# The doubling inverse of a chunked recurrence changes partition halves at some levels, and its turned update is issued between state and output products

## What is computed

```python
def rwkv7_scan(S0, r, decay, k, v, a_vec, b_vec):
    def step(S, inp):
        r_t, w_t, k_t, v_t, a_t, b_t = inp
        sa = jnp.einsum('bhvk,bhk->bhv', S, a_t)
        S = S * w_t[:, :, None, :] + sa[..., None] * b_t[:, :, None, :] + v_t[..., None] * k_t[:, :, None, :]
        return S, jnp.einsum('bhvk,bhk->bhv', S, r_t)
    xs = tuple(jnp.swapaxes(t, 0, 1) for t in (r, decay, k, v, a_vec, b_vec))
    S, ys = lax.scan(step, S0, xs)
    return jnp.swapaxes(ys, 0, 1), S
```

## Time and profile before

| what | us |
| --- | --- |
| median of 3 runs | 4411.86 |
| lowest, highest | 4408.74, 4422.03 |
| span of the profiled execution | 4419.8 |
| PE busy in it | 3990.1 (90%) |
| DVE busy in it | 2070.8 (47%) |
| ACT busy in it | 1727.3 (39%) |

### The profile page before, as it was taken

The page is one execution under the profiler, slowest core; times in us unless marked ns, Lnnn a source line. Parts: engine busy times, 40 slices in busy tenths (PEclk is TensorE's granted clock), DMA queues, the critical chain, the costliest instruction groups (busy, mean ns, idle before and its releaser), DMA issues.

```text
span 4419.8 us, 113544 instructions
## 1 busy us (share of the span) xinstructions
PE 3990.1 (90%) x49138; PEld 3475.0 (79%) x49138; DVE 2070.8 (47%) x4539; ACT 1727.3 (39%) x3547; POOL 519.2 (12%) x273
## 2 busy tenths in 40 slices
PE   7999999899968888879989999998999688888798
PEld 7999999788865565558989999997888565655587
DVE  6111112688845555555231111136787455565465
ACT  3000001577756665552110000026777465665421
POOL 5222221000000000002032222210000000000111
PEclk9999999999989999999999999999999899999899
DMA  3111112111124354344321111121111243543532
GB/s 141 73 63 73 73 73 79 46 52 52 37 59 148 112 177 135 91 145 153 112 72 73 73 73 73 69 81 40 51 48 37 81 158 90 176 139 108 175 128 79
DMA packets 227845, 410.47 MB, mean 93 GB/s; under 512 B 32786, under 2 KB 136980, under 8 KB 214292
## 3 DMA queue, kind: packets, MB, share of 16 engines
q1 hardware_dynamic: 213236, 320.15, 23.0%
q10 hardware_dynamic: 14112, 83.07, 4.7%
HBM read 296.39 MB, written 106.76 MB: 91 GB/s over the span
## 4 chain that ended last, share of the span: by engine, by line
PE 69%; DVE 10%; ACT 9%; issue 5%; PEld 3%; SPq 2%; DMA 2%; POOL 0%; ACTq 0%; DVEq 0%; PEldq 0%
PE psum L2251 11%; PE psum L2254 11%; PE psum L2253 11%; PE psum L1419 5%; PE psum L1447 4%; PE psum L762 3%; PE psum L1435 2%; PE psum L1183 2%; ACT arena L1223 2%; PE psum L1753 2%; PE psum L1754 2%; PE psum L1755 2%; PE psum L833 1%; PE psum L1175 1%; PE psum L759 1%
## 5 line engine op out<-in xcount | busy, mean ns | idle before, releaser
L2251 PE MATMUL psum<-x_hi,w_parts 128*128 128x416 f32 x2640 | 933.0, 353 | 42.8 <-POOL w_parts L2134 18.6
L2254 PE MATMUL psum<-x_hi,w_parts 128*128 128x416 f32 x2640 | 934.6, 354 | 0.0
L2253 PE MATMUL psum<-x_lo,w_parts 128*128 128x416 f32 x2624 | 918.5, 350 | 0.0
L2150 DVE TENSOR_TENSOR arena<-psum,arena 128x416 f32<-128x416 f32 x330 | 195.0, 592 | 1196.1 <-PE psum L2254 1192.3
L2251 PEld LDWEIGHTS psum<-x_hi,w_parts 128*128 128x128 f32 x2640 | 498.0, 189 | 52.6 <-POOL w_parts L2134 20.3
L375 ACT ACTIVATE arena<-arena 128x256 f32<-128x256 f32 x16 | 8.0, 501 | 1329.4 <-POOL arena L2138 1329.4
L2253 PEld LDWEIGHTS psum<-x_lo,w_parts 128*128 128x128 f32 x2624 | 494.9, 189 | 8.9 <-issue 0.6
L2254 PEld LDWEIGHTS psum<-x_hi,w_parts 128*128 128x128 f32 x2640 | 497.3, 188 | 3.4
L1326 DVE TENSOR_SCALAR_CACHE_REDUCE arena<-psum 128x512 f32<-128x512 f32 (+3 forms) x640 | 357.5, 607 | 287.7 <-PE psum L1419 155.3
L1419 PE MATMUL psum<-arena 64*128 64x512 f32 (+3 forms) x1280 | 329.4, 619 | 41.1 <-DVE arena L1326 22.4
L1447 PE MATMUL psum<-arena 128*128 128x128 f32 x2176 | 307.1, 282 | 64.0 <-ACT arena L1232 46.8
(11 more groups left out here) (348 smaller groups left out, 6754.8 us busy)
## 6 DMA issues: line engine op xcount, KB each, us to landing
arena<-in_cache_k SPq DMA_DIRECT2D x256, 256.0 KB, 2.9
arena<-in_cache_v SPq DMA_DIRECT2D x256, 256.0 KB, 3.0
out_proj_t<-arena ACTq DMA_DIRECT2D x60, 1040.5 KB, 4.1
arena<-in_w_in SPq DMA_DIRECT2D x66, 512.0 KB, 3.5
arena<-out_proj_t SPq DMA_DIRECT2D x96, 257.0 KB, 3.5
arena<-out_proj_t SPq DMA_DIRECT2D x24, 1024.0 KB, 6.2
x_res<-in_x SPq DMA_DIRECT2D x10, 1664.0 KB, 12.4
m_raw<-mixed_t SPq DMA_DIRECT2D x8, 1664.0 KB, 10.8
```

Of the source, the lines that this page charges most:

```text
L2150: dve.tensor_tensor(ost[:, b % 2, 1 + g * TG:1 + (g + 1) * TG], bank[PB[q % 7]][:, 0:TG], RSTD[:, cols(g)], ALU.mult).then_inc(p_ev, 1)
L2251: pe.matmul(bank[PB[q % n]][:, 0:TG], w_hi[:, b % 3, k, :], x_hi[:, g, k, :], start=(k == 0), stop=False)
L2253: pe.matmul(bank[PB[q % n]][:, 0:TG], w_hi[:, b % 3, k, :], xl, start=False, stop=False)
L2254: mm = pe.matmul(bank[PB[q % n]][:, 0:TG], w_lo[:, b % 3, k, :], x_hi[:, g, k, :], start=False, stop=(k == KT - 1))
```

## The change

It does four things.

1. The inverse of a unit may now lie in the other partition half. `side = (0, 1, 1, 0, 1, 0)` gives for each level whether XT lies in the half of before (0) or in the other (1). It flips after levels 0, 2, 3 and 4. Where it flips, the turned update has its rows in one half and its columns in the other, so it runs on the quarters (0,1) and (1,0).
2. `x_made` takes a function `beside` and calls it after every second unit of the turned update. `z_made(0)` goes with level 2, `z_made(1)` with level 3, `out_tokens` with level 4. The three have the quarters (0,0) and (1,1).
3. `z_made(1)` thereby moves behind the second `turned` and the first product of level 3. `z_made(0)` and `out_tokens` stay where they were, but for the turned update beside them.
4. On DVE the second `z_new` moves behind four steps of preparation (`sV_KF`, `sV_RKB`, `sV_MX`, `sV_RC`).

The number of matmuls, of copies and of transfers stays the same.

```diff
@@ rwkv_vector @@
                 if u is not None:
                     masked(u, 3)
+                if m is not None:
+                    for k in (sV_KF, sV_RKB, sV_MX, sV_RC):
+                        prep_vector(dve, m, k)
                 if t is not None:
                     z_new(t, 1)
                     zV.close()
-                if m is not None:
-                    for k in (sV_KF, sV_RKB, sV_MX, sV_RC):
-                        prep_vector(dve, m, k)
@@ rwkv_tensor @@
+            side = (0, 1, 1, 0, 1, 0)
+            half = lambda v, h, j: hs(j ^ h ^ side[v])
+            iy = lambda v, c, h: 4 * (h ^ side[v]) + c
...
-                    mm = pe.matmul(b8(h)[at(h, j), c, :], BS[hs(j), u % 3, ix(c, h), 2, :], X[hs(j), u % 2, ix(c, h), :], start=True, stop=True)
+                    mm = pe.matmul(b8(h ^ side[v])[half(v, h, j), c, :], BS[hs(j), u % 3, ix(c, h), 2, :], X[hs(j), u % 2, iy(v - 1, c, h) if v else ix(c, h), :], start=True, stop=True)
...
-            def x_made(u, v):
+            def x_made(u, v, beside=None):
...
-                for c, h, j in units:
-                    mm = pe.matmul(b8(2)[at(h, j), ix(c, h), :], Yp[at(h, j), ix(c, h), :], XT[at(h, j), u % 2, ix(c, h), :], start=True, stop=True)
-                xtT.inc(mm)
+                for i, (c, h, j) in enumerate(units):
+                    mm = pe.matmul(b8(2)[half(v + 1, h, j), ix(c, h), :], Yp[half(v, h, j), iy(v, c, h), :], XT[half(v, h, j), u % 2, ix(c, h), :], start=True, stop=True)
+                    if i == len(units) - 1:
+                        xtT.inc(mm)
+                    if beside and i % 2:
+                        beside(i // 2)
...
+                if t is not None:
+                    z_made(t, 0, u, 2)
+                elif u is not None:
                     x_made(u, 2)
-                if t is not None:
-                    z_made(t, 0)
...
                 if u is not None:
                     y_made(u, 3)
-                if t is not None:
-                    z_made(t, 1)
-                    zT.close()
...
-                if u is not None:
+                if t is not None:
+                    z_made(t, 1, u, 3)
+                    zT.close()
+                elif u is not None:
                     x_made(u, 3)
...
+                if t is not None:
+                    out_tokens(t, u)
+                elif u is not None:
+                    x_made(u, 4)
                 if u is not None:
-                    x_made(u, 4)
                     xT.close()
                     xtT.close()
-                if t is not None:
-                    out_tokens(t)
```

More of the change, by code:

```diff
@@ L758, in x_made @@
                     for c, h, j in units:
-                        mm = pe.matmul(b8(h)[hs(j), 4 + c, :], XT[at(h, j), u % 2, ix(c, h), :], Yp[at(h, j), ix(c, h), :], start=True, stop=True)
+                        mm = pe.matmul(b8(h ^ side[v])[hs(j), 4 + c, :], XT[half(v, h, j), u % 2, ix(c, h), :], Yp[half(v, h, j), iy(v, c, h), :], start=True, stop=True)
                     xT.inc(mm)
-                for c, h, j in units:
-                    mm = pe.matmul(b8(2)[at(h, j), ix(c, h), :], Yp[at(h, j), ix(c, h), :], XT[at(h, j), u % 2, ix(c, h), :], start=True, stop=True)
-                xtT.inc(mm)
+                for i, (c, h, j) in enumerate(units):
[4 more added lines that the diff above has]
+                        beside(i // 2)
             def scores(n, src, made):
@@ L798, in z_local, with z_made @@
                 zLoc.inc(mm)
-            def z_made(t, j):
+            def z_made(t, j, u=None, v=None):
                 i = 2 * t + j
@@ L808, in z_made, with two @@
                     zV.wait(pe, t - 1, 2)
[L809 to L813, removed]
+                def two(n):
+                    k, c = divmod(n, 4)
+                    for h in range(2):
+                        mm = pe.matmul(b8(4 + j)[hs(h), c, :], GQ[hs(h), j, c, 0:CH] if k else ident[hs(h), hs(h)], Z[hs(h), i % 3, c, :], start=False, stop=(k == 1), skip_group_check=True)
+                    if n == 7:
+                        zT.inc(mm)
+                if u is None:
+                    for n in range(8):
+                        two(n)
+                else:
+                    x_made(u, v, two)
             def out_state(t, n):
@@ L824, in out_state, with out_tokens, four @@
                 ySt.inc(mm)
-            def out_tokens(t):
+            def out_tokens(t, u=None):
                 ySt.wait(pe, t, 1)
                 ySt.close()
-                for k in range(2):
-                    for c, h, j in units:
+                def four(n):
+                    for c, h, j in units[4 * (n % 4):4 * (n % 4) + 4]:
                         i = ix(c, h)
-                        lhs, rhs = (BS[hs(j), t % 3, i, 1, :], WU[hs(j), i, CH:P]) if k else (SK[hs(j), t % 3, i, 0, :], VT[hs(j), t % 3, i, :])
-                        mm = pe.matmul(b8(6 + h)[hs(j), c, :], lhs, rhs, start=False, stop=(k == 1), skip_group_check=True)
-                yAll.inc(mm)
+                        lhs, rhs = (BS[hs(j), t % 3, i, 1, :], WU[hs(j), i, CH:P]) if n >= 4 else (SK[hs(j), t % 3, i, 0, :], VT[hs(j), t % 3, i, :])
+                        mm = pe.matmul(b8(6 + h)[hs(j), c, :], lhs, rhs, start=False, stop=(n >= 4), skip_group_check=True)
+                    if n == 7:
+                        yAll.inc(mm)
+                if u is None:
+                    for n in range(8):
+                        four(n)
+                else:
+                    x_made(u, NL - 1, four)
                 yAll.close()
```

1 line of the change is left out of this document (removed).

## The result

The changed kernel is slower: 4437.66 us median (4435.39 to 4452.07, 6 runs) against 4415.55 (4408.74 to 4428.7, 6 runs). The ratio is 1.0052, with a 95% interval of 1.0036 to 1.0068. The forecast was 4397 us, 0.34% faster, and its range ended at 4417. The profiled execution has a span of 4449.5 us, 12 above the median of its six runs. That of before, 4419.8, lies 4.3 above the median of its six, so the two spans differ by more (29.7 us) than the two medians (22.1).

What follows compares the result with a forecast made beforehand. The prediction took a chain alternating between PE and ACT/DVE to bound the recurrence; 2 + 3 + 26.4 - 2.8 - 5.7 - 8 = 14.9 us gained, from 4411.9 to 4397 us, range 4380 to 4417.

Steps and rivals of the forecast that it cites:

- The bound: Recurrence: ACT alone sets the 6.3 us from the copy of XT to L531; PE's saving there becomes waits.
- The first rival: PE bounds everywhere in the recurrence, all three merges pay 2.8 us in each of 30 slots: 84 us, 4328 us; chance 0.04.
- Quarters: Merged groups on both diagonals overlap: 1.04 us at level 2, 1.86 in place of 2.74 at level 4.
- Parts 1 and 3: Level 2 with `z_made(0)`: XT copy 0.1 us later, 2.8 us lost; level 4 with `out_tokens`: 0.88 us a slot, 26.4 gained.
- Part 2, slot 15: Level 3 with `z_made(1)`: in slot 15 the chain is PE's, 1.5 us gained in each layer, 3 us together.
- Part 4: Second `z_new` on DVE behind L531 delays the chain 0.34 or 0.19 us a slot: 5.7 us lost.
- my fourth rival: DVE gets later than counted, sliding into the next slot's first mask: 0.4 us a full slot, 10 us, 4407 us; chance 0.07.
- Part 5: Supply of PE's instructions: denser small matmuls stall by "issue" 0.27 us a slot more, 8 us lost.
- The rival "the supply is a ceiling": Some 31 instructions a us is all the supply allows, so nothing is gained: 4405 to 4415 us; chance 0.24.
- The slower rival: The two streams of a merged group do not overlap in the array, XT comes 1.03 us later: 4442 us; chance 0.05.

Runs made afterwards that it cites:

- e6: Kernel before with only the output products merged beside level 4, and identity half of state products as 2 matmuls of 256 columns, not 8 of 64: 4405.29 us, 0.9962.
- e9: Kernel before with one edit, the identity half of the state products as 2 matmuls of 256 columns in place of 8 of 64: 4408.05 us, ratio 0.9979.
- e11: Changed kernel with identity state products as 2 matmuls of 256 columns, not 8 of 64, and the second `z_new` back in its old place: 4458.07 us, 1.0092.
- e2: Changed kernel with only the output products merged, at level 4; state products and the second `z_new` in their old places: 4427.49 us, ratio 1.0001 to before.
- e1: Changed kernel with only the halves changed; all three groups of products stand apart and the second `z_new` is in its old place: 4424.42 us, 0.9998 to before.
- e8: Kernel before with the preparation's products cut along their columns, 26 matmuls more a full slot: 4491.21 us, ratio 1.016.
- e3: Changed kernel with only the state products merged, at levels 2 and 3; output products apart behind level 4: 4459.17 us, ratio 1.0064 to before.
- e4: Changed kernel with the second group of transposes issued twice, falling into PE's wait for L531: 4447.27 us, ratio 1.0056 to before.
- e5: Changed kernel with the identity half of the state products as 2 matmuls of 256 columns in place of 8 of 64: 4414.66 us, ratio 0.9998 to before.
- e7: Changed kernel with wide identity products, and output products as 8 matmuls of 256 columns, not 32 of 64, altering outputs: 4405.65 us, 0.9961 to before.
- e10: Changed kernel with 32 small matmuls added ahead of each recurrence, to move packet boundaries: 4472.48 us, ratio 1.0118 to before.

## Why the prediction was wrong

**The bound (right).** ACT's list sets the stretch between the copy of XT and L531: 6.32 us before and after. PE's saved 2 us there became waits for L461 and L531, where I had put them. The first rival, PE bounds everywhere, is refuted.

**Quarters (right).** 1.07 and 1.82 us against 1.04 and 1.86 forecast. One step was off: an instruction does not hold its quarter for the same 58 ns in both patterns, it is 0.52 / 8 = 65 ns with all four at work, and 16 x 65 is the 1.04. The Trainium skill's rule (TensorE: Matmul & The Clock Gate, Part 3, "What overlaps and what doesn't") is that a weight load overlaps only with matmuls of another row group. As the prediction worked it out, that would have given 1.96 and 2.74; the trace does not agree.

**Parts 1 and 3 (right in kind, part 3 too large).** Where nothing stalls, a slot with the low-rank part takes 29.24 us in place of 29.56, and level 4 with all behind L724 takes 7.71 in place of 8.25, the 0.54 that I had computed (0.88 - 0.34). But over all full slots level 4 was worth 0.41 us a slot even with the supply eased (e6 to e9), about half of the 0.88.

**Part 2, slot 15 (wrong in the second layer).** 2.5 us were gained in the first layer, more than the 1.5 forecast, and 3.8 lost in the second.

**Part 4 (undersized).** The 0.34 us are there: PE waits 0.4 us before the turned update of level 4 in 7 of 12 slots, and in e6 and e11, which have the second new state in its old place, once. (The view names L837, but in slot 10 that had ended at 1147.30, and the mask of level 4 on DVE at 1147.64, right before L766.) And DVE carries them on into the next slot: PE's wait for the mask L571 before `x_made` is 4.4 us in 12 slots in the changed kernel, 3.2 with the old place in e9 and 1.9 in e6. `y_made(2)` to the copy of XT grew by 0.2 us where I had 0.1. That is my fourth rival, at a quarter of its price: 0.1 us a slot, 2 to 3 us in all.

**Part 5 (the step that failed).** I allowed 8 us of stalls. The issue waits of PE in the two recurrences grew by 20 us, from 26 to 46. I had the right mechanism, had seen it in rows 2, 8 and 10, and took a price from the mean of the full slots of before. In the full slots alone they grew by 16.6 us, 0.69 a slot where I had 0.27, and that is more than the gain there (24 x 0.32 = 7.7). My guess is that the mean was low because large matmuls lay between the dense groups and gave the supply time; no run shows it. The rate that the supply sustains was visible in the slots without preparation, 2.9 us of stalls a slot, and I put that aside. The rival "the supply is a ceiling" came closest in kind, slots at full clock are at 29.92 us as before, but its 4405 to 4415 us was passed too. Nor is it a fixed rate: slot 10 runs 920 instructions in 29.24 us, 31.5 a us, with no stall.

**The clock (missing from the sum).** All rows of before stood at 1.00, and I took that as given. I had even computed that PE would stand still 2.5 us a slot in new places and called it free. Stalls of 1 to 2 us and these waits together took the clock down in 7 of 24 full slots, at an estimated 3 to 11 us, and again in the late ones. It adds to the loss. Whether it decides the sign is not shown: in the full slots the stalls alone grew by more than the gain.

**The slower rival** had the wrong mechanism. I gave it 0.05 for two streams that don't share the array; they do.

In sum, for the recurrences of the profiled executions: +17.3 us, of which the full slots are 24 x (30.38 - 29.93) = 10.8, the four late slots 6.2 and slot 0 the rest. Of the forecast's 24 slots x 0.44 us = 10.6 us of gain in the full slots some 8 were made, if all gained the 0.32 of slot 10 (an estimate), and they were spent on stalls.

What stays open: why a packet comes late at some places more than at others, and what exactly in the state merges makes a stall cost the clock. The runs narrow the second. e2 kept the stalls (44 us) without the waits for L461 and with short ones for L531, and one full slot fell, not 7. Taken together, in the six kernels whose state products stand apart (before, e1, e2, e6, e8, e9) 19 "issue" stalls of 1 us or more lie in full slots, and the clock fell within 4 us behind one of them. In the seven with the state merges (the changed kernel, e3, e4, e5, e7, e10, e11) it was 26 of 54. So a stall costs the clock mostly where the merges have also left PE idle elsewhere. Waits alone did it in e11. No run took apart the wait for L461 and the merged groups themselves, and each count comes from one profiled execution of each kernel.

## What to carry to other kernels

Time that an engine saves in a stretch that another engine sets is not neutral: it becomes idle time, and here idle time of TensorE also cost the clock of what followed (in e11, behind 12 of 24 waits of up to 2.4 us). Where thousands of small matmuls run at 15 to 30 ns each, count instructions as a resource beside array time: merging groups saves array time and not one instruction, while one wide matmul in place of four narrow ones with the same weights saves instructions, and here cost nothing (e9: 0.9979). Look at the "issue" waits of the densest slots before you price such a merge, and try it together with the saving in instructions.

## What the runs showed of the hardware

- Sixteen fp32 products of 64 x 64 on one diagonal of quarters and sixteen on the other, interleaved two by two, take 1.07 us; on one diagonal alone sixteen take 0.93.
- Each of 122 stalls by "issue" of 0.8 us or more ended 2.2 to 2.9 us after the start of a 16 KB transfer of PE's instructions (all profiles, full slots).
- Which slots stall depends on where the 16 KB packets of PE's instructions end: half a packet of shift exchanged long and short slots (28 to 33 us) of nearly equal work.
- 12 matmuls fewer of 460 a slot were worth 0.5% of the whole kernel where the supply was short (e5 to the changed kernel), and 0.2% where it was less so (e9 to before).
- The granted clock fell from 2.4 to 1.2 GHz behind 26 of 54 stalls of 1.0 to 2.3 us in kernels whose state products are merged, behind 1 of 19 of 1.0 to 1.7 us where they stand apart, behind 12 of 24 waits of up to 2.4 us (e11) and behind none of 86 waits of 1.0 to 1.6 us.
- 32 matmuls of 64 columns into the same place took 13.5 us, 0.42 us each, at a granted clock of 0.52 (e10).
